# Eight experts in 144 equal weight units instead of 160, with longer rows and an unrolled loop

## The chip, the cores and the metric

One Trainium2 chip, of which one NeuronCore runs the whole kernel. The metric is the device time of one execution in microseconds (us). The kernel before ran three times: 1297.24, 1297.76 and 1300.47 us, median 1297.76 us.

## The reference

A decoder trunk of two layers makes one step for 256 prompt tokens and 8 sample tokens, 264 in all, with D = 1024. Each layer has a mixer (one wide projection, a gated linear recurrence, a short convolution, an output projection), a feed-forward part and a gated per-layer embedding. The feed-forward part of layer 0 is a dense SwiGLU; that of layer 1 sends each token to 2 of 8 experts:

```
logits = n2 @ router                      # 264 x 8, float32
top_v, top_i = top_k(logits, 2);  top_w = softmax(top_v)
for e in range(8):                        # w_gu[e]: 1024 x 3072, w_dn[e]: 1536 x 1024, float32
    g, u = split(n2 @ w_gu[e], 2)
    out += comb[:, e:e+1] * ((silu(g) * u) @ w_dn[e])
```

All weights are float32 in HBM. One expert has 18 MB of them (12 MB gate and up, 6 MB down).

## The kernel before

Each weight matrix comes through SBUF in units of at most 1 MB. A unit has four steps, each in order on one engine. SyncE (SP) issues its DMA into a raw slot (`load`, L282 to L292) as soon as that slot's last unit has been converted. ScalarE makes its float16 upper half (`hi`, L827, `wh <- raw`). VectorE makes its float16 remainder (`lo`, L1129, `wl <- raw, wh`). TensorE multiplies three times for each pair of tiles: upper by upper, upper by lower half of the activations, remainder by upper. `wh` and `wl` have four slots, so that a unit is converted at most three units ahead of TensorE (`LEAD`): `hi` of unit n + 3 waits until TensorE is done with unit n - 1.

The expert part runs from about 745 us of the profile to 1240. Before it a routing chain ranks the logits. Each expert then has a table of up to 96 tokens (`CAP`): a one-hot matrix `sel` (VectorE, L1565) gathers their activations by matmul from `nt`, where the 264 tokens lie on partitions in tiles of 128, 128 and 8 (L720, 48 matmuls). A loop (`Fori`) over the experts, one body on each engine, holds per expert:

- 12 gate and up units of 1 MB, 256 columns of all 1024 rows, so 1 KB runs in HBM. Each is 48 matmuls with 96 moving columns (L753 to L755), read out by ScalarE (L1078, L1079, L1082) and multiplied by VectorE in four operations for every two units (L1469 to L1475).
- then the gather for the next expert (L720), which TensorE runs ahead of
- 8 down units of 768 KB, 512 columns of 384 rows, 2 KB runs, 9 matmuls of 512 columns each (L782 to L784). The first four make the left half of the output, the last four the right.
- the output rows, scaled by the routing weight (`ye`: L1098 on ScalarE, L1641 on VectorE), which TensorE scatters back to the 264 tokens (L733, L735) while the next expert's gate and up units run; VectorE adds them to the residual (L1614, eight adds).

The first turn scatters zeros, and the last gathers once more for nobody: nine gathers, eight of use. Five raw slots hold the units (four of `raw`, and `xb`). The four loads of the PLE matrix that follows the experts wait for the four units before each. A pass for tables that overflow is branched over.

Of the kernel before, what the change touches and what calls it, by code (L numbers as in the profile page):

```python
# [12 lines left out]
P = 128  # L13
# [13 lines left out]
MOE_SLOTS = SLOTS + 1  # L27
# [21 lines left out]
MOE_EVAC = MOE_GU + 2  # L49
UNCOUNTED = NE * (MOE_U - MOE_EVAC)  # L50
# [35 lines left out]
def moe_unit_size(u):  # L86
    return UNIT if u % MOE_U < MOE_GU else DN_K * 512


def program(nc, a, o):  # L90

    ctx = ExitStack()
    with ctx:
# [52 lines left out]
        spare = sb("spare", [1, 5])  # L146
        csr = sb("csr", [P, 2])
        csl = sb("csl", [P, 1])
# [8 lines left out]
        raw_slot = [raw[:, i] for i in range(SLOTS)] + [xb[:].rearrange("p c t -> p (c t)")[:, 0:UNIT]]  # L157
# [13 lines left out]
        hid_e = w1_half[:, 0:2 * EC * CAP].rearrange("p (s c t) -> p s c t", s=2, c=EC)  # L171
        at = 2 * EC * CAP
# [3 lines left out]
        xg = ga[:].rearrange("p a c t -> p (a c t)")[:, 0:2 * C * CAP].rearrange("p (s c t) -> p s c t", s=2, c=C)  # L176
        sel = ga[:].rearrange("p a c t -> p (a c t)")[:, 2 * C * CAP:2 * C * CAP + 3 * CAP].rearrange("p (t n) -> p t n", t=3)
        ye = gb[:].rearrange("p a c t -> p (a c t)")[:, 0:2 * D].rearrange("p (s n) -> p s n", s=2)
        sel_t = gb[:].rearrange("p a c t -> p (a c t)")[:, 2 * D:2 * D + T]
# [11 lines left out]
        pair_u, pair_w = pair2[:, 0], pair2[:, 1]  # L191
        plew = side[:].rearrange("p a c n -> p (a c n)").rearrange("p (k n) -> p k n", k=PC)
# [28 lines left out]
        selt_full = sem("selt_full")  # L221
        sp_sel, sp_gat, sp_x, sp_csl = sem("sp_sel"), sem("sp_gat"), sem("sp_x"), sem("sp_csl")
# [40 lines left out]
        def _(sp):  # L263
# [66 lines left out]
            n0 = N_MOE  # L330
            gu = a["moe_w_gu"][0].rearrange("e (c p) m -> p e c m", p=P)
            dn = a["moe_w_dn"][0].rearrange("e (c p) m -> p e c m", p=P)
            sp.wait_ge(hi_done, N_MOE)
            sp.wait_ge(lo_done, N_MOE)
            with sp.Fori(0, NE) as e:
                for u in range(MOE_GU):
                    if u == SLOTS:
                        sp.wait_ge(aux_full, AX_LGT)
                        sp.wait_ge(xn_ready, 4 * 5)
                    col = (u % 2) * FE + (u // 2) * 256  # L340
                    load(n0 + u, gu[:, bass.ds(e, 1), :, col:col + 256].rearrange("p e c m -> p (e c) m"),
                         u % MOE_SLOTS, C, e, MOE_U, MOE_SLOTS)
                for u in range(MOE_DN):
                    half, k = u // 4, u % 4 * DN_K
                    src = dn[:, bass.ds(e, 1), k:k + DN_K, half * 512:(half + 1) * 512]
                    load(n0 + MOE_GU + u, src.rearrange("p e c m -> p (e c) m"), (MOE_GU + u) % MOE_SLOTS, DN_K, e,
                         MOE_U, MOE_SLOTS)
# [97 lines left out]
        def _(pe):  # L445
# [153 lines left out]
            def ple(l, n):  # L599
                norm_stats()  # L600
                pe.wait_ge(side_loaded, 16 * 5 * (l + 1))
                if l:
                    pe.wait_ge(sc_done, 8 * NE + 16)
# [29 lines left out]
            for t, (lo, n) in enumerate(TOK):  # L633
                last = nc.tensor.transpose(bank[0:n, t * NE:(t + 1) * NE], lgt[:, lo:lo + n], ident[0:NE, 0:NE])
            last.then_inc(aux_full, 1)

            def rows_of_tokens(s):

                for t, (lo, n) in enumerate(TOK):
# [10 lines left out]
            for t, (lo, n) in enumerate(TOK):  # L650
                last = nc.tensor.transpose(bank[0:NE, lo:lo + n], rank[0:n, t, :], ident[0:n, 0:n])
# [4 lines left out]
            for t, (lo, n) in enumerate(TOK):  # L656
                nc.tensor.transpose(bank[0:n, t * NE:(t + 1) * NE], cum[:, lo:lo + n], ident[0:NE, 0:NE])
# [5 lines left out]
            def slots_by_token(bank):  # L663

                for t, (lo, n) in enumerate(TOK):
# [4 lines left out]
            with pe.If(spilled > 0):  # L670

                with pe.Fori(0, SPILLS) as p:
                    with pe.Fori(0, NE) as e:
# [3 lines left out]
                        for c in range(C):  # L677
                            bank = aux[:, c // 4, (c % 4) * CAP:(c % 4 + 1) * CAP]
                            for i in range(6):
                                t, n = i // 2, TOK[i // 2][1]  # L680
# [31 lines left out]
            def gather(adds):  # L712

                for g in range(4):
                    pe.wait_ge(sc_done, adds(g + 5))
                    for c in (2 * g, 2 * g + 1):
                        for s in range(2):
                            at = (c % 2 * 2 + s) * CAP
                            for t, (_, n) in enumerate(TOK):
                                last = nc.tensor.matmul(aux[:, g, at:at + CAP], nt[0:n, s, t, c * P:(c + 1) * P],  # L720
                                                        sel[0:n, t, :], start=(t == 0), stop=(t == 2))
                    if g == 3:
                        for t, (_, n) in enumerate(TOK):
# [4 lines left out]
            def scatter(chunks, free):  # L728

                for c in chunks:  # L730
                    if free:
                        free(c)
                    nc.tensor.matmul(aux[:, c % 4, 0:T], ye[0:CAP, 0, c * P:(c + 1) * P], sel_t[0:CAP, :],  # L733
                                     start=True, stop=False)
                    nc.tensor.matmul(aux[:, c % 4, 0:T], ye[0:CAP, 1, c * P:(c + 1) * P], sel_t[0:CAP, :],  # L735
                                     start=False, stop=True).then_inc(sc_full, 1)

            pe.wait_ge(sel_ready, 1)
            gather(lambda i: i)
            with pe.Fori(0, NE) as e:  # L740
                pe.wait_ge(gat_done, e * 4 + 4)
                for u in range(MOE_GU):
                    n = N_MOE + u
                    pe.wait_ge(evac_done, e * MOE_EVAC + (n - 1))
                    pe.wait_ge(hi_done, e * MOE_U + (n + 1))
                    pe.wait_ge(lo_done, e * MOE_U + (n + 1))
                    th = wh[:, u % SLOTS, :].rearrange("p (c m) -> p c m", c=C)
                    tl = wl[:, u % SLOTS, :].rearrange("p (c m) -> p c m", c=C)
                    for m in range(2):
                        bank = acc[:, u % 2, m * CAP:(m + 1) * CAP]  # L750
                        for k in range(C):
                            hi, lo = th[:, k, m * P:(m + 1) * P], tl[:, k, m * P:(m + 1) * P]
                            nc.tensor.matmul(bank, hi, xg[:, 0, k, :], start=(k == 0), stop=False)  # L753
                            nc.tensor.matmul(bank, hi, xg[:, 1, k, :], start=False, stop=False)  # L754
                            last = nc.tensor.matmul(bank, lo, xg[:, 0, k, :], start=False, stop=(k == C - 1))  # L755
                    last.then_inc(unit_mm, 1)
                    if u == 1:
                        pe.wait_ge(ys_ready, e * 2 + 2)
                        pe.wait_ge(selt_ready, e + 1)
                        scatter(range(4), None)  # L760
                    if u in (4, 6):
                        scatter(range(u, u + 2), lambda i: pe.wait_ge(sc_done, e * 8 + (8 + i - 3)))
                    if u == 7:
                        pe.wait_ge(sc_done, e * 8 + (8 + 5))
                        slots_by_token(aux[:, 0, :]).then_inc(selt_full, 1)
                pe.wait_ge(sel_ready, e + 2)
                gather(lambda i: e * 8 + (i + 8))
                for u in range(MOE_DN):
                    n = N_MOE + MOE_GU + u
                    half, k0 = u // 4, u % 4 * DN_K  # L770
                    pe.wait_ge(hi_done, e * MOE_U + (n + 1))
                    pe.wait_ge(lo_done, e * MOE_U + (n + 1))
                    if k0 == 0:
                        pe.wait_ge(ys_ready, e * 2 + (half + 1))
                    th = wh[:, u % SLOTS, 0:DN_K * 512].rearrange("p (c m) -> p c m", c=DN_K)
                    tl = wl[:, u % SLOTS, 0:DN_K * 512].rearrange("p (c m) -> p c m", c=DN_K)
                    for k in range(DN_K):
                        if half == 0 and (k0 + k) % 2 == 0:
                            pe.wait_ge(hid_ready, e * 6 + (FFN_IT * 2 + (k0 + k) // 2 + 1))
                        bank = acc[0:CAP, 2 + half, :]  # L780
                        first, end = k0 + k == 0, k0 + k == EC - 1
                        nc.tensor.matmul(bank, hid_e[:, 0, k0 + k, :], th[:, k, :], start=first, stop=False)  # L782
                        nc.tensor.matmul(bank, hid_e[:, 0, k0 + k, :], tl[:, k, :], start=False, stop=False)  # L783
                        last = nc.tensor.matmul(bank, hid_e[:, 1, k0 + k, :], th[:, k, :], start=False, stop=end)  # L784
                    last.then_inc(unit_mm, 1)

            pe.wait_ge(selt_ready, NE + 1)
# [897 lines left out]
```

## Time and profile before

| | us |
|---|---|
| median of the three runs | 1297.76 |
| the profiled execution, span | 1300.5 |
| first gather of the expert part starts | 745.26 |
| last down matmul starts | 1239.63 |
| ScalarE reads the next norm's sum | 1257.05 |
| busy TensorE / VectorE / ScalarE | 1219.6 / 1021.0 / 746.0 |

The span is that of the profiled execution, within 0.03 us of the slowest of the three runs. A busy TensorE includes matmuls that overlap; the distance between starts tells its pace. In the page's 40 slices each slice is 32.5 us, so slices 24 to 38 are the expert part.

### The profile page before, as it was taken

To read this page: it belongs to the slowest core of one execution; us is meant where nothing else is said; L and a number is where in the kernel's file an instruction comes from. 1 tells how busy PE (TensorE), PEld (TensorE's weight loads), DVE (VectorE), ACT (ScalarE), POOL (GpSimd) and SP (SyncE) were. 2 spreads that over 40 slices of the span, in tenths; PEclk is the share of its full clock that TensorE was granted. 3 is DMA by queue.
4 is the path that set the end of the run, shared out by engine and by line. 5 is a ranking of instruction groups with operands and counts; after the bars stand their busy time and mean duration, and the time that the engine had idled before them with its cause. 6 is when DMAs were issued, how large, how long until landed. Compare 5 with 4: busy or idle time off the path is not lost.

```text
span 1300.5 us, 30219 instructions
## 1 busy us (share of the span) xinstructions
PE 1219.6 (94%) x12256; PEld 981.2 (75%) x12256; DVE 1021.0 (79%) x1203; ACT 746.0 (57%) x802; POOL 24.9 (2%) x59
## 2 busy tenths in 40 slices
PE   8999999999999998999999789897979798989888
PEld 4888888788888887888888476767666666767656
DVE  5977877876666689868867768979797978889875
ACT  5556644465554464466443575767676675858543
POOL 3000000000000010000000000000000000000000
PEclk9999999999999999999999988989898898989889
DMA  9675655646566543655654558989899999989720
GB/s 251 195 245 176 204 190 192 195 149 200 190 201 198 194 146 131 209 180 181 208 198 129 163 180 273 355 274 331 286 322 294 316 301 322 295 294 337 259 83 34
DMA packets 257298, 288.66 MB, mean 222 GB/s; under 512 B 5451, under 2 KB 230747, under 8 KB 257226
## 3 DMA queue, kind: packets, MB, share of 16 engines
q1 hardware_dynamic: 255514, 283.71, 67.4%
q0 software_dynamic: 1728, 4.16, 1.2%
q8 instruction: 40, 0.66, 0.2%
q14 instruction: 16, 0.13, 0.0%
HBM read 286.53 MB, written 1.52 MB: 221 GB/s over the span
## 4 chain that ended last, share of the span: by engine, by line
PE 67%; DVE 19%; issue 8%; ACT 4%; DMA 2%; DVEq 1%; ACTq 0%; SPq 0%
PE acc L496 14%; PE acc L498 14%; PE acc L497 14%; DVE wl L1129 9%; PE aux L720 5%; ACT wh L827 2%; PE acc L782 2%; PE acc L783 2%; PE acc L784 2%; PE acc L481 2%; PE acc L482 2%; PE acc L488 2%; DVE h L1614 1%; PE acc L753 1%; PE acc L755 1%
## 5 line engine op out<-in xcount | busy, mean ns | idle before, releaser
L1129 DVE SCALAR_TENSOR_TENSOR wl<-raw,wh 128x2048 f16<-128x2048 f32 (+1 forms) x252 | 548.8, 2186 | 165.9 <-ACT wh L827 163.0
L827 ACT ACTIVATE wh<-raw 128x2048 f16<-128x2048 f32 (+1 forms) x252 | 459.7, 1825 | 101.8 <-PE acc L784 61.8
L496 PE MATMUL acc<-xn,wh 128*128 128x264 f16 x1424 | 393.0, 276 | 0.8 <-DVE wl L1129 0.8
L498 PE MATMUL acc<-xn,wl 128*128 128x264 f16 x1424 | 393.0, 276 | 0.0
L497 PE MATMUL acc<-xn,wh 128*128 128x264 f16 x1424 | 393.0, 276 | 0.0
L753 PE MATMUL acc<-ga,wh 128*128 128x96 f16 x1536 | 210.0, 209 | 40.2 <-DVE wl L1129 26.4
L755 PE MATMUL acc<-ga,wl 128*128 128x96 f16 x1536 | 210.4, 210 | 0.0
L754 PE MATMUL acc<-ga,wh 128*128 128x96 f16 x1536 | 210.1, 210 | 0.0
L753 PEld LDWEIGHTS acc<-ga,wh 128*128 128x128 f16 x1536 | 153.3, 100 | 48.8 <-issue 44.3
L496 PEld LDWEIGHTS acc<-xn,wh 128*128 128x128 f16 x1424 | 139.3, 98 | 21.9 <-ACT wh L827 1.0
L497 PEld LDWEIGHTS acc<-xn,wh 128*128 128x128 f16 x1424 | 139.3, 98 | 21.1
L498 PEld LDWEIGHTS acc<-xn,wl 128*128 128x128 f16 x1424 | 139.3, 98 | 20.9
L754 PEld LDWEIGHTS acc<-ga,wh 128*128 128x128 f16 x1536 | 153.5, 100 | 0.9
L755 PEld LDWEIGHTS acc<-ga,wl 128*128 128x128 f16 x1536 | 153.6, 100 | 0.0
L862 ACT ACTIVATE ot<-acc 128x528 f32<-128x528 f32 x47 | 28.6, 610 | 124.2 <-PE acc L498 97.3
L782 PE MATMUL acc<-wh,w 128*96 128x512 f16 x192 | 80.3, 418 | 0.0
L783 PE MATMUL acc<-wl,w 128*96 128x512 f16 x192 | 79.4, 414 | 0.0
L784 PE MATMUL acc<-wh,w 128*96 128x512 f16 x192 | 78.9, 411 | 0.0
L1129 DVE SCALAR_TENSOR_TENSOR wl<-xb,wh 128x2048 f16<-128x2048 f32 (+1 forms) x32 | 64.6, 2020 | 4.2 <-ACT wh L827 4.2
L720 PE MATMUL aux<-ga,w 128*128 128x96 f16 (+1 forms) x432 | 62.1, 251 | 3.4 <-issue 3.4
L827 ACT ACTIVATE wh<-xb 128x2048 f16<-128x2048 f32 (+1 forms) x32 | 54.3, 1697 | 14.8 <-DMA xb<-in_moe_w_gu 9.8
L720 PEld LDWEIGHTS aux<-ga,w 128*128 128x128 f16 (+1 forms) x432 | 32.3, 103 | 32.7 <-issue 3.5
(268 smaller groups left out, 1611.0 us busy)
## 6 DMA issues: line engine op xcount, KB each, us to landing
raw<-in_moe_w_gu SPq DMA_DIRECT2D x80, 1024.0 KB, 8.4
raw<-in_w_in SPq DMA_DIRECT2D x56, 1024.0 KB, 5.1
raw<-in_moe_w_dn SPq DMA_DIRECT2D x48, 768.0 KB, 5.9
raw<-in_ffn_w_gu SPq DMA_DIRECT2D x24, 1024.0 KB, 5.2
xb<-in_moe_w_gu SPq DMA_DIRECT2D x16, 1024.0 KB, 8.6
raw<-in_ffn_w_dn SPq DMA_DIRECT2D x12, 1024.0 KB, 5.3
xb<-in_moe_w_dn SPq DMA_DIRECT2D x16, 768.0 KB, 6.0
raw<-in_w_a_out SPq DMA_DIRECT2D x8, 1024.0 KB, 5.1
```

What stands on the lines that cost most here:

```text
L496: nc.tensor.matmul(bank, hi, x[:, 0, x0 + k, :], start=(k == 0), stop=False)
L497: nc.tensor.matmul(bank, hi, x[:, 1, x0 + k, :], start=False, stop=False)
L498: last = nc.tensor.matmul(bank, lo, x[:, 0, x0 + k, :], start=False, stop=(k == k_chunks - 1))
L720: last = nc.tensor.matmul(aux[:, g, at:at + CAP], nt[0:n, s, t, c * P:(c + 1) * P], sel[0:n, t, :], start=(t == 0), stop=(t == 2))
L753: nc.tensor.matmul(bank, hi, xg[:, 0, k, :], start=(k == 0), stop=False)
L754: nc.tensor.matmul(bank, hi, xg[:, 1, k, :], start=False, stop=False)
L755: last = nc.tensor.matmul(bank, lo, xg[:, 0, k, :], start=False, stop=(k == C - 1))
L782: nc.tensor.matmul(bank, hid_e[:, 0, k0 + k, :], th[:, k, :], start=first, stop=False)
L783: nc.tensor.matmul(bank, hid_e[:, 0, k0 + k, :], tl[:, k, :], start=False, stop=False)
L784: last = nc.tensor.matmul(bank, hid_e[:, 1, k0 + k, :], th[:, k, :], start=False, stop=end)
L827: nc.scalar.activation(wh[:, s, 0:size], raw_slot[from_slot][:, 0:size], ACT.Copy, scale=WS).then_inc(hi_done, 1)
L1129: op(V.scalar_tensor_tensor(out=wl[:, s, 0:size], in0=raw_slot[raw_turn(n)[0]][:, 0:size], scalar=WS, in1=wh[:, s, 0:size], op0=ALU.mult, ...
```

## The change

An expert becomes 18 units of 1 MB. A gate or up unit is now 512 columns of 512 rows (2 KB runs), and two such units fill one PSUM bank with four blocks of 96 columns; a down unit is all 1024 columns of 256 rows (4 KB runs), 12 matmuls, both halves of the output together. There are six raw slots (`ya` is added). The token tiles of the expert part are 88, 88 and 88 (`MTOK`). The loop over experts is written out, with constant wait values. The gather of the next expert comes after its predecessor's second down unit, into a second copy of `xg`; the four VectorE operations for two units become two on VectorE for four units, a copy on ScalarE and a subtraction on VectorE, all 384 wide. The first turn scatters nothing and there are eight gathers. The PLE loads wait for the unit six before each. POOL's queue is not touched; on SP the wait for all earlier conversions ahead of the expert loads is gone.

```diff
-MOE_SLOTS = SLOTS + 1
+MOE_SLOTS = 6
-FFN_IT, MOE_GU, MOE_DN = FF // 512, 2 * FE // 256, 8
+FFN_IT, MOE_GU, MOE_DN = FF // 512, 12, 6
-DN_K = EC // 4
+GU_K, DN_K = C // 2, 2
+RT = T // 3
+MTOK = ((0, RT), (RT, RT), (2 * RT, RT))
-        raw_slot = [raw[:, i] for i in range(SLOTS)] + [xb[:].rearrange("p c t -> p (c t)")[:, 0:UNIT]]
+        raw_slot = [raw[:, i] for i in range(SLOTS)] + [x[:].rearrange("p c t -> p (c t)")[:, 0:UNIT] for x in (ya, xb)]
...
-            def load(n, src, slot, k, it=None, step=0, slots=SLOTS):
+            def load(n, src, slot, k, it=None, step=0):
+                slots = MOE_SLOTS if n >= N_MOE + SLOTS else SLOTS
...
-                    sp.wait_ge(hi_done, n - LEAD)
-                    sp.wait_ge(lo_done, n - LEAD)
+                    sp.wait_ge(hi_done, n + 1 - slots)
+                    sp.wait_ge(lo_done, n + 1 - slots)
...
-            sp.wait_ge(hi_done, N_MOE)
-            sp.wait_ge(lo_done, N_MOE)
-            with sp.Fori(0, NE) as e:
+            for e in range(NE):
                 for u in range(MOE_GU):
...
+                    k, col = u % 2 * GU_K, u // 2 % 2 * FE + u // 4 * 512
+                    moe_load(gu_unit(e, u), gu[:, e, k:k + GU_K, col:col + 512], GU_K)
+                for d in range(MOE_DN):
+                    moe_load(dn_unit(e, d), dn[:, e, d * DN_K:(d + 1) * DN_K, :], DN_K)
...
-                            for t, (_, n) in enumerate(TOK):
+                            for t, (_, n) in enumerate(MTOK):
                                 last = nc.tensor.matmul(aux[:, g, at:at + CAP], nt[0:n, s, t, c * P:(c + 1) * P],
                                                         sel[0:n, t, :], start=(t == 0), stop=(t == 2))
...
+            def gate_or_up(e, u):
+                n, s = gu_unit(e, u), u % 2
+                group = GROUPS * e + u // 4
+                if s == 0 and group:
+                    pe.wait_ge((gate_out, up_out)[u // 2 % 2], group)
+                if u < 2:
+                    pe.wait_ge(gat_done, 4 * e + 2 * u + 2)
+                pe.wait_ge(hi_done, n + 1)
+                pe.wait_ge(lo_done, n + 1)
...
+                for m in range(4):
+                    bank = acc[:, u // 2 % 2, m * CAP:(m + 1) * CAP]
+                    for k in range(GU_K):
...
+            for e in range(NE):
                 for u in range(MOE_GU):
+                    gate_or_up(e, u)
+                    if e and u in (2, 4):
+                        scatter(e - 1, range(2 * u - 4, 2 * u))
+                for d in range(MOE_DN):
+                    down(e, d)
+                    if e + 1 < NE and d == 1:
+                        pe.wait_ge(sel_ready, e + 2)
+                        gather(e + 1)
+                    if e + 1 < NE and d == 2:
+                        selected_slots(e + 1)
+            keep_warm(14)
+            scatter(NE - 1, range(C))
...
+            def down(e, d):                       # ScalarE
+                n = dn_unit(e, d)
+                hi(n + LEAD)
+                if d == 0:
+                    hidden_hi(GROUPS * e + GROUPS - 1)
+                if d == MOE_DN - 1:
+                    act.wait_ge(unit_mm, n + 1)
+                    act.wait_ge(csl_ready, e + 1)
...
-            op(V.memset(ye[0:CAP], 0.0), ys_ready, 2)
-            op(V.memset(sel_t[0:CAP, :], 0.0), selt_ready)
...
+            def gate_or_up(e, u):                 # VectorE
+                n, q = gu_unit(e, u), GROUPS * e + u // 4
+                lo(n + LEAD)
+                if u in (4, 8):
+                    hidden_lo(q - 1)
+                if u % 4 == 3:
...
+                    op(V.scalar_tensor_tensor(out=moe_w[:, b, :], in0=moe_t[:, b, :], scalar=1.0, in1=moe_g[:, b, :],
+                                              op0=ALU.add, op1=ALU.mult))
+                    settle()
+                    op(V.scalar_tensor_tensor(out=moe_w[:, b, :], in0=moe_w[:, b, :], scalar=0.5 * XS,
+                                              in1=moe_u[:, b, :], op0=ALU.mult, op1=ALU.mult), hid_w)
```

## Rows read from the trace of the kernel before

**Rows 1.** The page: granted clock and busy DMA share in 40 slices.

```profile
PEclk9999999999999999999999988989898898989889
DMA  9675655646566543655654558989899999989720
```

**Rows 2.** TensorE's gathers for experts 0, 1 and the last (x48), and the last down matmuls.

```profile
745.26 7.41 PE L720 MATMUL aux<-ga,w 128*128 128x96 f16 x48 [3.37 <-issue]
...
788.66 6.10 PE L720 MATMUL aux<-ga,w 128*128 128x96 f16 x48
...
1216.15 6.42 PE L720 MATMUL aux<-ga,w 128*128 128x96 f16 x48
...
1239.42 0.38 PE L783 MATMUL acc<-wl,w 128*96 128x512 f16 x1
1239.63 0.38 PE L784 MATMUL acc<-wh,w 128*96 128x512 f16 x1
```

**Rows 3.** Stretches: length, busy us by engine, granted clock, DMA share, GB/s.

```profile
870.00:896.00 26.00, 22.63 (x418) 19.72 (x415) 25.28 (x26) 20.59 (x22) 0.00 (x0) 1.00 1.10 348
897.00:901.00 4.00, 2.61 (x62) 2.49 (x60) 3.90 (x5) 3.41 (x7) 0.00 (x0) 1.00 1.07 379
862.00:864.00 2.00, 2.00 (x11) 1.11 (x10) 1.33 (x2) 1.48 (x1) 0.00 (x0) 1.00 0.00 1
908.30:921.90 13.60, 13.60 (x80) 7.44 (x78) 8.17 (x16) 3.23 (x5) 0.00 (x0) 0.50 0.90 305
```

**Rows 4.** ScalarE (start us, us, instruction): gate/up conversions, a down conversion, a gather readout.

```profile
886.53 1.91 ACT L827 ACTIVATE wh<-raw 128x2048 f16<-128x2048 f32 x1 [0.88 <-DMA raw<-in_moe_w_gu]
...
889.54 1.91 ACT L827 ACTIVATE wh<-raw 128x2048 f16<-128x2048 f32 x1 [0.67 <-DMA raw<-in_moe_w_gu]
...
859.66 1.48 ACT L827 ACTIVATE wh<-raw 128x1536 f16<-128x1536 f32 x1 [7.01 <-PE acc L784]
...
790.31 0.48 ACT L1061 ACTIVATE ga<-aux 128x384 f16<-128x384 f32 x1
```

**Rows 5.** VectorE in order of time, one of each kind.

```profile
755.49 2.29 DVE L1129 SCALAR_TENSOR_TENSOR wl<-raw,wh 128x2048 f16<-128x2048 f32 x1 [1.46 <-ACT wh L827]
760.51 2.29 DVE L1129 SCALAR_TENSOR_TENSOR wl<-xb,wh 128x2048 f16<-128x2048 f32 x1 [2.73 <-ACT wh L827]
...
847.39 0.62 DVE L1565 TENSOR_SCALAR ga<-iota,pos 128x96 f16<-128x96 f32 x3
...
872.73 4.48 DVE L1129 SCALAR_TENSOR_TENSOR wl<-raw,wh 128x2048 f16<-128x2048 f32 x2
877.13 0.74 DVE L1641 SCALAR_TENSOR_TENSOR gb<-acc,csl,gb 96x512 f16<-96x512 f32 x1
886.65 0.77 DVE L1614 SCALAR_TENSOR_TENSOR h<-aux,h 128x264 f32<-128x264 f32 x2
1271.64 0.70 DVE L1457 SCALAR_TENSOR_TENSOR ya<-ot,ya 128x528 f32<-128x528 f32 x1
```

**Rows 6.** TensorE matmul starts at full clock (784) and at half clock (909).

```profile
784.12 0.21 PE L755 MATMUL acc<-ga,wl 128*128 128x96 f16 x1
784.16 0.21 PE L753 MATMUL acc<-ga,wh 128*128 128x96 f16 x1
...
909.29 0.28 PE L754 MATMUL acc<-ga,wh 128*128 128x96 f16 x1
909.37 0.28 PE L755 MATMUL acc<-ga,wl 128*128 128x96 f16 x1
```

**Rows 7.** Instruction packets by queue (packets, MB, share of 16 engines): page, then 746:800.

```profile
q8 instruction: 40, 0.66, 0.2%
...
q8 instruction: 7, 0.11, 0.9%
```

**Rows 8.** ScalarE after the last expert.

```profile
1242.21 1.91 ACT L827 ACTIVATE wh<-raw 128x2048 f16<-128x2048 f32 x1 [1.10 <-DMA raw<-in_w_ple_gate]
1257.05 0.48 ACT L848 ACTIVATE std<-aux,eps 128x264 f32<-128x264 f32 x1 [10.84 <-PE aux L536]
```

More of the change, by code:

```diff
@@ L637, in rows_of_tokens @@
             def rows_of_tokens(s):
[L639 removed]
+                for t, (lo, n) in enumerate(MTOK):
                     bank = aux_bank().bitcast(F16)
@@ L710, in _, with gather @@
                 pe.nop()
-            def gather(adds):
+            def gather(e):
                 for g in range(4):
-                    pe.wait_ge(sc_done, adds(g + 5))
+                    if e == 1:
+                        pe.wait_ge(gat_done, g + 1)
+                    if e > 1:
+                        pe.wait_ge(sc_done, 8 * (e - 2) + 4 + g + 1)
+                    if e and g == 0:
+                        pe.wait_ge(selt_ready, e)
                     for c in (2 * g, 2 * g + 1):
@@ new lines, in down @@
+            def down(e, d):
+                n = dn_unit(e, d)
+                pe.wait_ge(hi_done, n + 1)
+                pe.wait_ge(lo_done, n + 1)
+                if d == 0 and e:
+                    pe.wait_ge(ys_ready, 2 * e)
+                if d % 2 == 0:
+                    pe.wait_ge(hid_ready, 2 * FFN_IT + GROUPS * e + d // 2 + 1)
+                th = wh[:, n % SLOTS, :].rearrange("p (c m) -> p c m", c=DN_K)
+                tl = wl[:, n % SLOTS, :].rearrange("p (c m) -> p c m", c=DN_K)
+                for k in range(DN_K):
+                    at = (d * DN_K + k) * CAP
+                    x_hi, x_lo = (hid_e[:, e % 2, i, at:at + CAP] for i in range(2))
+                    for half in range(2):
+                        cols = slice(half * 512, (half + 1) * 512)
+                        bank = acc[0:CAP, 2 + half, :]
+                        nc.tensor.matmul(bank, x_hi, th[:, k, cols], start=(d == 0 and k == 0), stop=False)
+                        nc.tensor.matmul(bank, x_hi, tl[:, k, cols], start=False, stop=False)
+                        last = nc.tensor.matmul(bank, x_lo, th[:, k, cols], start=False,
+                                                stop=(d == MOE_DN - 1 and k == DN_K - 1))
+                last.then_inc(unit_mm, 1)
@@ L738, in _ @@
+            pe.wait_ge(evac_done, N_MOE)
             pe.wait_ge(sel_ready, 1)
-            gather(lambda i: i)
-            with pe.Fori(0, NE) as e:
-                pe.wait_ge(gat_done, e * 4 + 4)
+            gather(0)
+            selected_slots(0)
+            for e in range(NE):
                 for u in range(MOE_GU):
[L743 to L785, printed above, removed]
@@ new lines, in down @@
+            def down(e, d):
+                n = dn_unit(e, d)
+                hi(n + LEAD)
+                if d == 0:
+                    hidden_hi(GROUPS * e + GROUPS - 1)
+                if d == MOE_DN - 1:
+                    act.wait_ge(unit_mm, n + 1)
+                    act.wait_ge(csl_ready, e + 1)
+                    if e:
+                        act.wait_ge(sc_full, 8 * e)
+                    for half in range(2):
+                        nc.scalar.activation(ye[0:CAP, 0, half * 512:(half + 1) * 512], acc[0:CAP, 2 + half, :],
+                                             ACT.Identity, scale=csl[0:CAP, e % 4:e % 4 + 1]).then_inc(ye_hi, 1)
@@ L1100, in _ @@
+            gathered(0)
+            selected_slots(0)
+            for e in range(NE):
+                for u in range(MOE_GU):
+                    gate_or_up(e, u)
+                for d in range(MOE_DN):
+                    down(e, d)
+                    if e + 1 < NE and d == 2:
+                        gathered(e + 1)
+                    if e + 1 < NE and d == 3:
+                        selected_slots(e + 1)
             ple(1, N_PLE[1])
@@ new lines, in down @@
+            def down(e, d):
+                n = dn_unit(e, d)
+                lo(n + LEAD)
+                if d == 0:
+                    hidden_lo(GROUPS * e + GROUPS - 1)
+                if d == MOE_DN - 1:
+                    for half in range(2):
+                        s = slice(half * 512, (half + 1) * 512)
+                        vec_e.wait_ge(ye_hi, 2 * e + half + 1)
+                        op(V.scalar_tensor_tensor(out=ye[0:CAP, 1, s], in0=acc[0:CAP, 2 + half, :],
+                                                  scalar=csl[0:CAP, e % 4:e % 4 + 1], in1=ye[0:CAP, 0, s],
+                                                  op0=ALU.mult, op1=ALU.subtract), ys_ready)
@@ L1644, in expert @@
-                settle()
-                vec_e.wait_ge(gat_done, e * 4 + 8)
-                slot_weights()
-            run_loop(NE, {lo_done: MOE_U, dv: 2 * 6 + 3 + 1, pair_free: 6, hid_ready: 6, ys_ready: 2, sc_done: 8,
-                          sel_ready: 1, csl_ready: 1}, expert)
+                for d in range(MOE_DN):
+                    down(e, d)
+                    if e + 1 < NE and d == 4:
+                        slot_weights(e + 1)
             for c in range(C):
-                add_scattered(c, lambda i: NE * 8 + i)
+                add_scattered(NE - 1, c)
```

238 lines of the change are left out of this document (122 added, 116 removed).

## The prediction

> **What bounds the kernel now.** I read the page's slices first. Through the routing TensorE runs with a granted clock near full and DMA engines about half busy; in the expert part the DMA share rises to 8 and 9 tenths, but not to a steady 9, and the clock dips once per expert [rows 1]. So something there is periodic. The gathers give the period: from 788.66 to 1216.15 are seven experts, 61.07 us each [rows 2].
>
> Next I cut one period into stretches [rows 3]. In the gate and up units DMA is saturated: share 1.10, 348 GB/s. There VectorE is busy 25.28 of 26 us, nearly full too. ScalarE says which of them ends last: it starts a unit every 3.01 us and each time waits 0.67 to 0.88 us for the DMA [rows 4]. 1.0486 MB at 348 GB/s is 3.01 us, so this part goes at the pace of 1 KB runs. In the down part ScalarE waits 7.01 us for TensorE [rows 4], no slot comes free, and DMA stands still (1 GB/s from 862 to 864 [rows 3]). TensorE there works through a gather of 6.1 to 6.4 us [rows 2] and the first down units at half clock: 908.3 to 921.9 is granted 0.50 (1.2 of 2.4 GHz) with TensorE busy 13.6 of 13.6 us [rows 3]. So an expert is a DMA-bound stage and a TensorE-bound stage one after the other, with little overlap between them. Twelve units at 3.01 are 36.1 us, eight of 0.786 MB at 379 GB/s would be 16.6, sum 52.7: some 8.4 us of the 61.07 are idle DMA.
>
> **The change part by part.**
>
> *Rows and units.* The 2 KB runs of today's down units reach 379 GB/s where the queue is full [rows 3]. The new gate and up units have such runs; down units have 4 KB runs, which no row shows alone. I price all 18 at 379: 2.77 us each, 49.8 per expert. Bounds: no gain from longer runs, 3.01 us; and for the 4 KB runs the step from 1 to 2 KB once more, 2.54 us, worth 6 x 0.23 = 1.4 per expert. I take 379, as the row of the same run length for two thirds of the bytes. The sixth slot keeps DMA at most six units ahead of VectorE.
>
> The Trainium skill, DMA: Bandwidth & Descriptors (Specifications and Bandwidth), gives about 358 GB/s as what HBM grants one core, which would speak against this gain: by it a unit takes 2.93 us, an expert 52.7, as an estimate. The trace shows 379 over 4 us, above that figure, so I keep the row.
>
> *VectorE.* Two conversions back to back take 4.48 us, the second starting 2.20 after the first (4.48 - 2.29 + overlap) [rows 5]. Per expert: 18 x 2.20 = 39.6. Hidden values: nine operations 384 wide (two multiplies and a subtraction for each of three groups); two 264-wide ones take 0.77 together and a 528-wide one 0.70, so about 0.55 each, 5.0 (bounds 9 x 0.39 = 3.5 and 9 x 0.70 = 6.3; 384 lies halfway). Four pairs of adds at 0.68 (0.77 less overlap): 2.7. Two output halves at 0.74: 1.5. The one-hot 0.62 [rows 5] and three tiny operations, together 1.2 as an estimate. Sum 50.0 us.
>
> *ScalarE.* 18 conversions at 1.91 are 34.4; nine readouts, three new copies and the gather's four, all 384 wide, at 0.48 [rows 4] add 7.7, the rest some 2: 44, below 50, so the moved copy costs nothing while VectorE or DMA is later. If it were not, it would cost 3 x 0.48.
>
> *TensorE.* The same counts, 576 gate/up and 72 down matmuls. At full clock gate/up starts are 0.04 apart [rows 6], so 23 us; down starts 0.21 apart [rows 2], 72 x 0.21 = 15.1; scatter about 2, 16 matmuls of 264 columns. The gather is 48 matmuls in 6.10 us at mostly full clock, 0.127 each, although a gate/up matmul of the same 96 columns takes 0.04. Every third one is on the 8-token tile; with three equal tiles of 88 I expect no such break and the gate/up pace: 48 x 0.04 = 1.9, between that and no gain, 6.1. Sum 42 to 46 us, below VectorE. The gather now stands after two down units; behind it on TensorE wait four down units, and ScalarE has three units converted ahead (5 to 8 us of work for TensorE), so its pause of 2 to 6 us is covered by them. If they are not there, it costs its length, as today.
>
> *New waits.* Scatter and `xg` wait for the readout of the next gather, which ended some 10 us earlier. TensorE's single-step transposes (`selected_slots`) wait one readout of 0.5 us per expert; behind it stand four down units, and I cost it at nothing for the same cover.
>
> *Unrolling.* Today's loop body is fetched once: seven 16 KB instruction packets in 746 to 800 [rows 7] and none later in the expert part. Written out, each expert fetches its own, seven times eight. Page: 40 packets are 0.2% of 16 engines' 1300.5 us, 1.04 us each. If all lie on one DMA engine, it loses 7.3 us per expert, and a unit has landed only when its slowest engine is done; if they spread, 0.45. No row names the engine. I take the middle, 3.6, since in 746 to 800 DMA waits on ScalarE were no more than half a microsecond above those of rows 4. So DMA: 49.8 + 3.6 = 53.4 per expert, 2.97 per unit.
>
> The Trainium skill, Runtime: NRT & Kernel Launch (Instruction fetch mechanics), has a taken branch break the fetch ahead and prefers unrolled code. The trace disagrees for this loop: no packet after its first turn. By the rule unrolling would gain a stall per turn; by the row it only adds packets.
>
> *The sum, on the profile's clock.* (a) First gather at 745.26, 7.41 us at half clock [rows 2]; 48 matmuls at 0.08 [rows 6] are 3.9, so all that follows it starts 3.5 earlier; VectorE's first expert conversion 755.49 [rows 5] becomes 752.0. (b) The pipeline fills: 4 us idle, as 1.46 and 2.73 before its first two conversions now [rows 5]. (c) VectorE then has 141 conversions, 310.2, and 8 x 5.0 + 7 x (2.7 + 1.5 + 1.2) = 78: its last ends at 1144, and TensorE's last unit of 2.6 at 1147. That is the floor. (d) DMA: after 18 conversions and the rest of expert 0, at 802, it can be six units ahead, at unit 26; 117 more at 2.97 end at 1149.5; conversion in two steps and the last unit, 1.9 + 2.2 + 2.6, end at 1156. So DMA is last by 9 us. (e) For half-clock stretches and the two near-equal streams meeting I add 6 us, from nothing to 8 x 6.8 = 54 (each of today's half-clock stretches of 13.6 losing half): the last down matmul ends at 1162, against 1239.9 now [rows 2]. (f) From there to the next norm's sum are 17.2 us now, with ScalarE's conversions of the PLE units waiting 1.1 us and more for loads in front of the second output half [rows 8]. These loads now start two units, some 5.5 us, sooner: I take 4, from 0 to 5.5. Sum: 78 + 4 = 82 off 1300.5: 1218.5. The median lies 2.7 below the profiled execution: 1216 us.
>
> **The rivals.**
> 1. *One engine's extra packets, or runs that gain nothing.* For it: a landing needs all 16 parts. Full 7.3 per expert: 3.17 per unit, 802 + 371 + 6.7 = 1180, with no allowance (e), since a DMA that is last by so much covers it: 18 later than 1162, so 1234. With 3.01 for every run and half the packets: 3.21, 1185, so 1239. Against: the 379 row. 1228 to 1245. By the figure of the Trainium skill (DMA: Bandwidth & Descriptors, Specifications) a unit would take 2.93 + 0.2, the stage end at 1175 and the run take 1229, the near end of this case.
> 2. *The half clock stays where it is.* For it: a gate/up unit holds TensorE 2.0 of some 2.9 us, as loose as now, and in the period of rows 3 the clock fell at the end of that stage (908.3, gather at 909); then down units take 5.1 us instead of 2.6. Per expert 13.6 us at half clock lose 6.8, and if nothing covers it period 58 to 60: 1162 + 8 x 6 = 1210, so 1264. Against: three units of cover, and the thin gather gone.
> 3. *TensorE stays at half clock through the gate/up units: slower.* Place: L753's successors, 576 x 0.08 = 46 us, with down, gather and scatter at full clock 66 per expert, above 61.07: 8 x 4.9 = 39 more in the stage, 7.5 back at its ends, 1329. It decides from 60% of the period at half clock (43 us of work plus half of 36); in rows 3 it is 13.6 of 61.07. Against: at half clock those units would leave no idle time, and after a busy stretch (908.3 to 921.9) the clock came back.
> 4. *It doesn't do what it says:* the sixth slot and longer runs wait behind TensorE's order as today: 1290 to 1300. Against: the idle DMA follows from gather and half clock, which change.
>
> **How the numbers follow.** Forecast 1200 to 1228: 0.58. Rival 1, 1228 to 1245: 0.20. Rival 2, 1245 to 1290: 0.13. Rival 4, 0.04, half of it within 0.3%. Rival 3, 0.05. Range 1198 to 1246, which leaves out rivals 2 to 4 and a part below the floor. Under 0.3%, 4 us, nothing could be told from no change. Faster 0.93, same 0.02, slower 0.05.
>
> **What would show it.** The gather's 48 matmuls in 2 to 4 us (from 6); the rate in gate/up stretches near 379 from 348; about 56 more instruction packets; gathers 52 to 55 us apart; no DMA standstill in the down units; VectorE busy over 90% of an expert. It would be wrong if ScalarE still waited several microseconds for TensorE in each expert, if waits for DMA grew past 0.9 us, or if half clock held through the gate/up units.

## The result, and the profile after

The changed kernel takes 1238.05 us (median of four runs, 1235.05 to 1239.42) against 1299.08 of the kernel before: ratio 0.9522, 95% interval 0.9500 to 0.9544. That is faster, inside the forecast range, and 22 us above the predicted 1216. It lies in the time band of rival 1, which blamed DMA; the profile shows that DMA was not the cause. The profiled execution took 1235.05 us, its span is 1233.4.

The page of the changed kernel, granted clock and DMA share in 40 slices of 30.8 us, and the instruction queues (packets, MB, share of 16 engines), against [rows 1, 7]:

```profile
PEclk8999999999999999999999998999989898989989
DMA  9675665646556654465565626999899998989900
...
q8 instruction: 79, 1.29, 0.4%
q14 instruction: 23, 0.18, 0.0%
```

The DMA share is steadier than in [rows 1], but the clock still dips in the expert part. TensorE's first gather of the expert part and a later one, the last down matmul, and then ScalarE's read of the next norm's sum, against [rows 2, 8]:

```profile
744.16 4.00 PE L739 MATMUL aux<-ga,w 88*128 88x96 f16 x48 [3.40 <-issue]
...
1054.66 2.21 PE L739 MATMUL aux<-ga,w 88*128 88x96 f16 x48
...
1173.98 0.38 PE L811 MATMUL acc<-wh,w 128*96 128x512 f16 x1
```

```profile
1188.85 0.48 ACT L887 ACTIVATE std<-aux,eps 128x264 f32<-128x264 f32 x1 [11.68 <-PE aux L550]
```

Behind the first, a gather takes 2.2 us where it took 6.1 to 7.45. Gathers 2 to 8 start at 782.8 to 1109.3, 54.4 us apart on average (before: 61.07).

One period of the changed kernel, cut into stretches as in [rows 3] (length, then busy us and count for PE, PEld, DVE, ACT and POOL, granted clock, DMA share, GB/s):

```profile
1012.00:1026.90 14.90, 12.41 (x255) 11.58 (x252) 14.83 (x13) 12.58 (x13) 0.00 (x0) 1.00 1.04 371
1026.90:1033.70 6.80, 4.24 (x40) 3.58 (x41) 5.72 (x7) 1.84 (x2) 0.00 (x0) 0.50 1.03 401
1033.70:1050.00 16.30, 14.24 (x312) 13.60 (x310) 12.63 (x16) 12.37 (x12) 0.00 (x0) 1.00 0.76 272
1050.00:1066.60 16.60, 16.34 (x119) 9.87 (x117) 16.09 (x10) 13.91 (x15) 0.00 (x0) 1.00 1.03 377
```

The gate/up units run at 371 GB/s (348 before), and the stretch with the gather and the down units, the last, is at full clock. The fault has moved to the middle of the gate/up units: 6.8 us at half clock, and behind them a stretch in which VectorE is busy 12.63 of 16.3 us and the DMA share falls to 0.76. The waits of the same period (engine, line, what for: us in total, times, longest) say who waits:

```profile
ACT w L1114 <- DVE sg L1695: 6.8, 3, 3.0
ACT sa L1126 <- PE acc L789: 5.9, 1, 5.9
PEld aux L763 <- DVE h L1673: 5.4, 2, 5.2
DVE wl L1188 <- ACT wh L866: 5.2, 2, 4.7
PE aux L763 <- DVE h L1673: 5.1, 1, 5.1
```

No row of that answer is a wait for a DMA. The first row is ScalarE waiting for VectorE, the slower of the two. The chain of waits puts the other four in order (start us, us, what):

```profile
1026.39 2.20 DVE wl L1188
1028.59 0.47 DVE w L1680
1029.06 0.35 DVE h L1673
1029.46 0.40 PE aux L763
...
1033.72 0.08 PE acc L789
1034.65 0.36 issue
1035.02 0.49 ACT sa L1127
1035.50 1.81 ACT wh L866
1037.33 2.21 DVE wl L1188
```

Read it from the top. TensorE finishes gate/up unit 4 (counted from 0) at 1024.4 and has the second half of the scatter (L763) next. That half writes the four `aux` banks of the first half, so it waits until VectorE has added the first half to `h` (L1673). VectorE comes to the adds only at 1029, after the conversions for units that lie up to three ahead. TensorE stands 5.1 us, its clock falls to half, and the unit behind the scatter takes 3.4 us (1031.2 to 1034.6) where the two units before it took 2.1 each. Meanwhile ScalarE and VectorE have used up their lead of three units, and VectorE then stands 4.7 us, its one long gap in the period: the 49.3 us that it is busy in the four stretches and its 5.2 us of waits make 54.5 of the 54.6 us of this period.

The kernel before had this wait too, but short: its adds stand in pairs after gate/up units 2, 3, 5 and 7, and its scatter in three pieces. TensorE's waits for the adds from 800 to 1150, in the kernel before:

```profile
PE aux L733 <- DVE h L1614: 8.4, 6, 1.6
```

and in the changed kernel:

```profile
PE aux L763 <- DVE h L1673: 34.5, 7, 5.1
```

### The profile page after: what moved, and what is told of

It is laid out like the page before. It is cut to its first block, busy times and chain, and to the rows that moved or that the text cites. A ratio compares the mean times of both kernels' runs of the same rounds, so it can differ in the third digit from the quotient of the medians.

```text
span 1233.4 us, 28154 instructions
## 1 busy us (share of the span) xinstructions
PE 1150.7 (93%) x12177; PEld 955.8 (77%) x12177; DVE 988.4 (80%) x1050; ACT 735.8 (60%) x730; POOL 24.9 (2%) x59
## 4 chain that ended last, share of the span: by engine, by line
PE 58%; DVE 32%; ACT 8%; issue 2%; DMA 0%; ACTq 0%; SPq 0%; DVEq 0%
DVE wl L1188 21%; PE acc L510 15%; PE acc L512 15%; PE acc L511 15%; ACT wh L866 5%; PE acc L495 2%; PE acc L502 2%; PE acc L496 2%; DVE h L1673 1%; DVE xb L1262 1%; PE aux L599 1%; DVE sg L1695 1%; DVE sg L1692 1%; PE aux L550 1%; DVE gb L1707 1%
## 5 line engine op out<-in xcount | busy, mean ns | idle before, releaser
L1188 DVE SCALAR_TENSOR_TENSOR wl<-raw,wh 128x2048 f16<-128x2048 f32 x220 | 501.7, 2288 | 141.2 <-ACT wh L866 140.3
L866 ACT ACTIVATE wh<-raw 128x2048 f16<-128x2048 f32 x220 | 418.1, 1906 | 4.5 <-PE acc L811 4.4
L786 PE MATMUL acc<-ga,wh 128*128 128x96 f16 x1536 | 207.6, 210 | 13.6 <-ACT wh L866 9.4
L788 PE MATMUL acc<-ga,wh 128*128 128x96 f16 x1536 | 207.2, 210 | 0.2 <-issue 0.2
L789 PE MATMUL acc<-ga,wl 128*128 128x96 f16 x1536 | 207.0, 209 | 0.4 <-issue 0.4
L809 PE MATMUL acc<-wh,w 128*96 128x512 f16 x192 | 73.2, 381 | 4.1 <-ACT wh L866 3.4
L810 PE MATMUL acc<-wl,w 128*96 128x512 f16 x192 | 72.8, 379 | 0.0
L811 PE MATMUL acc<-wh,w 128*96 128x512 f16 x192 | 72.8, 379 | 0.0
L1188 DVE SCALAR_TENSOR_TENSOR wl<-xb,wh 128x2048 f16<-128x2048 f32 x24 | 54.8, 2285 | 0.4 <-ACT wh L866 0.4
L1188 DVE SCALAR_TENSOR_TENSOR wl<-ya,wh 128x2048 f16<-128x2048 f32 x24 | 54.8, 2284 | 0.3 <-ACT wh L866 0.3
L763 PE MATMUL aux<-gb 96*128 96x264 f16 x64 | 20.6, 342 | 36.3 <-DVE h L1673 35.2
L866 ACT ACTIVATE wh<-ya 128x2048 f16<-128x2048 f32 x24 | 45.7, 1903 | 0.7 <-PE acc L789 0.7
```

The lines of the kernel that those rows point to most:

```text
L786: nc.tensor.matmul(bank, hi, x_hi, start=(s == 0 and m == 0 and k == 0), stop=False, skip_group_check=True)
L788: nc.tensor.matmul(bank, hi, x_lo, start=False, stop=False, skip_group_check=True)
L789: last = nc.tensor.matmul(bank, lo, x_hi, start=False, stop=end, skip_group_check=True)
L809: nc.tensor.matmul(bank, x_hi, th[:, k, cols], start=(d == 0 and k == 0), stop=False)
L810: nc.tensor.matmul(bank, x_hi, tl[:, k, cols], start=False, stop=False)
L811: last = nc.tensor.matmul(bank, x_lo, th[:, k, cols], start=False, stop=(d == MOE_DN - 1 and k == DN_K - 1))
```

## Experiments

Two theories stood against each other. Theory W (the wait of the scatter's second half): the place of the adds sets the period, through the scatter's wait, TensorE's stop and its clock. The rival: DMA, by fetch packets or run length, sets it, as rival 1 of the prediction has it. A third question was which part of the change made it faster at all.

**e1: the adds two units earlier.**

```diff
-                    if e and u in (4, 6):
-                        for c in range(2 * u - 8, 2 * u - 4):
+                    if e and u in (2, 5):
+                        for c in range(0, 4) if u == 2 else range(4, 8):
```

> VectorE's eight adds of the last expert come after gate/up units 2 and 5 instead of 4 and 6; nothing else changes. Theory W (the wait of the second scatter half for the first adds, 5.1 us in the trace of after, makes the one VectorE gap of 4.7 us per expert): the gap goes, 7 x 4.7 = 33 us, so 1203 to 1210 us, gathers 50 us apart, and no half clock after the scatter. Theory F (DMA with the packets of the unrolled code sets the pace near 53.4 per expert): ScalarE starts to wait for DMA and the time stays at 1228 or above. Theory C (the clock halves in any case because gate/up units are loose): half-clock stretches stay, 1220 to 1230.

Measured 1203.16 us (1202.11 to 1203.46), ratio 0.9256 (0.9240 to 0.9271): 34.9 below the changed kernel, from moving eight small instructions. The period is 49.77 us in every expert. The same stretch of time in the changed kernel:

```profile
800.00:1150.00 350.00, 301.00 (x4670) 248.41 (x4668) 314.26 (x276) 260.01 (x243) 0.00 (x0) 0.94 0.95 350
```

and in e1:

```profile
800.00:1150.00 350.00, 318.51 (x4941) 258.30 (x4938) 346.02 (x301) 282.37 (x262) 0.00 (x0) 1.00 1.01 372
```

VectorE goes from 314.26 to 346.02 busy of 350, the clock from 0.94 to 1.00. The scatter no longer stops TensorE; the first matmul of its second half follows the unit before it at once:

```profile
957.69 0.21 PE L789 MATMUL acc<-ga,wl 128*128 128x96 f16 x1
957.73 0.28 PE L763 MATMUL aux<-gb 96*128 96x264 f16 x1
```

Theory W holds. The run also bears out a term of the prediction: the period is VectorE's sum. DMA is busy all the time here too (share 1.01), but no row of the run's waits is for a DMA, so VectorE is the later of the two.

**e2: the stop stays, the clock does not fall.** Filler matmuls fill TensorE's wait.

```diff
+                    if e and u == 4:
+                        pe.wait_ge(ys_ready, 2 * e)
+                        for _ in range(24):
+                            nc.tensor.matmul(acc[:, 2, :], identh[:], identh[:, 0:1].to_broadcast([P, 512]),
+                                             start=True, stop=True)
```

> As after, but TensorE runs 24 filler matmuls of 512 columns (5.1 us at full clock) into a free bank just ahead of the second scatter half, in the time it waits anyway. Theory W says that the stop itself and the half clock that follows share the 4.7 us: at full clock the next gate is done some 1.5 to 2.5 us sooner, so 7 x 2 = 14 less, 1222 to 1230. If the half clock is the whole cause: 1203 to 1212. If it costs nothing: 1238.

Measured 1224.15 us (1223.19 to 1225.15), ratio 0.9422 (0.9407 to 0.9438). Waits from 800 to 1150:

```profile
ACT sa L1131 <- PE acc L789: 29.5, 7, 4.2
DVE wl L1193 <- ACT wh L871: 24.1, 13, 3.0
```

The period is 52.90, with full clock in all of it. Of the 4.64 us that the changed kernel loses per expert (54.41 less 49.77), 1.5 are the half clock and 3.1 the stop itself. Work that is useless but keeps TensorE busy paid here, though not as well as removing the stop.

**e3: the loop of the kernel before written out, nothing else.**

```diff
-            with pe.Fori(0, NE) as e:
+            for e in range(NE):
```

(likewise on SyncE, ScalarE and VectorE)

> The kernel before with nothing but its loop over the experts written out on all four engines. Theory F (all extra instruction packets on one DMA engine, about 1 us each): its DMA-bound gate/up units go from 3.01 to about 3.2 us, ScalarE's waits for DMA grow by 0.2 to 0.4 us each, 8 x 2.4 to 4.9 us, so 1318 to 1338. If packets spread or are absorbed: 1299 within 4. If loop turns cost something (register waits): up to 8 less, 1291.

Measured 1294.46 us (1292.00 to 1300.88, ten runs) against 1300.21, ratio 0.9959 (0.9944 to 0.9975): slightly faster. Instruction queue from 800 to 1140 in this kernel, where the kernel before has no packet:

```profile
q8 instruction: 32, 0.52, 0.7%
```

So the packets come, some six per expert, and cost nothing that can be measured; the fetch theory falls. The Trainium skill, Runtime: NRT & Kernel Launch (Instruction fetch mechanics), has a taken branch break the fetch ahead where its target is not in the two pages held; the kernel before fetches nothing from 800 to 1140, so no run here shows that stall. The 5.75 us gained, some 0.7 per turn, stay without a cause: the mean granted clock from 800 to 1150 is higher as well, 0.93 against 0.91.

**e4 and e5: four raw slots instead of six,** on the changed kernel and on e1.

```diff
-MOE_SLOTS = 6
+MOE_SLOTS = 4
...
```

> As after with four raw slots instead of six (the expert units use the same slots as the other matrices). Theory W: VectorE and the scatter wait set the pace, and three loads in flight of 2.7 us each still run ahead of a unit every 3.0 us: 1236 to 1246. Theory F (DMA is near the bound): DMA falls idle when a slot is late and cannot catch up, 1255 to 1290.

> The adds early (as e1) and four raw slots (as e4). If four slots cost e4's 18.8 us only by making the scatter wait longer (7.2 us there, from 5.2): with that wait gone nothing is left, 1203 to 1207 us. If they cost by idle DMA engines (ScalarE's waits for DMA of 0.6 to 1.7 us in e4): some 1.5 to 3 us per expert stay, 1214 to 1227.

e4 took 1256.86 us (1256.07 to 1260.05), ratio 0.9680 (0.9659 to 0.9700); e5 took 1224.04 (1221.11 to 1229.72), ratio 0.9422 (0.9385 to 0.9459). e4 is above the 1236 to 1246 that theory W had for it and inside the 1255 to 1290 of theory F, by which DMA falls idle when a slot is late and cannot catch up: a miss, as I had not counted that with four slots DMA becomes late too. e5 lies in the 1214 to 1227 of the reading by which idle DMA is what fewer slots cost. Waits of e4 from 800 to 1150:

```profile
PE aux L763 <- DVE h L1673: 40.9, 6, 7.1
...
ACT wh L866 <- DMA raw<-in_moe_w_gu: 22.9, 35, 1.4
```

and of e5:

```profile
ACT wh L866 <- DMA raw<-in_moe_w_gu: 36.5, 45, 3.1
```

The last two of the six slots are worth 19 us in the changed kernel and 21 in e1: with four, ScalarE waits for loads, with six no row of either run's waits is for a load. The kernel before had five slots, and no run prices the one that the change added.

**e6: one of the hidden operations from VectorE to GpSimd,** on e1.

```diff
+            for q in range(GROUPS * NE):
...
+                pool.wait_ge(hid_hi, q + 1)
+                nc.gpsimd.tensor_tensor(hid_e[:, r, 1, at:at + 4 * CAP], moe_w[:, q % 2, :],
+                                        hid_e[:, r, 0, at:at + 4 * CAP], ALU.subtract).then_inc(hid_ready, 1)
...
-                vec_e.wait_ge(hid_hi, q + 1)
-                op(V.tensor_tensor(hid_e[:, r, 1, at:at + 4 * CAP], moe_w[:, q % 2, :], hid_e[:, r, 0, at:at + 4 * CAP],
-                                   ALU.subtract), hid_ready)
...
```

> As e1, but the three hidden_lo subtractions of an expert (0.55 us each on VectorE) run on GpSimd. If VectorE's own work is now the bound (period 49.77, its sum was 50.0): it falls by 1.65, and DMA is next at some 48.4 (12 x 2.74 + 6 x 2.58): 8 x 1.4 = 11 less, 1190 to 1195. If DMA or ScalarE's waits for VectorE (L1114, 2.5 us each) already end last: 1201 to 1204. If GpSimd slows VectorE or its results come late: above 1204.

Measured 1206.62 us (1205.87 to 1207.04), ratio 0.9274 (0.9247 to 0.9301): 3.5 above e1, although VectorE has 3 x 0.55 us less to do per expert. GpSimd's operation, ScalarE's conversion behind the copy, and VectorE's two conversions beside them:

```profile
913.16 2.35 POOL L457 TENSOR_TENSOR w<-sg,w 128x384 f16<-128x384 f32 x1 [24.79 <-ACT w L1119]
```

```profile
912.99 1.90 ACT L871 ACTIVATE wh<-raw 128x2048 f16<-128x2048 f32 x1
```

```profile
912.45 2.28 DVE L1193 SCALAR_TENSOR_TENSOR wl<-raw,wh 128x2048 f16<-128x2048 f32 x1
914.92 2.73 DVE L1193 SCALAR_TENSOR_TENSOR wl<-raw,wh 128x2048 f16<-128x2048 f32 x1 [0.19 <-ACT wh L871]
```

The subtraction left VectorE's queue, but two things eat more than it took. VectorE now comes to its next conversion before ScalarE has converted that unit (until 914.89), and starts it 2.47 us behind the last one instead of 2.20. And it takes 2.73 us instead of 2.28, with GpSimd still running for its first 0.6 us. Together that is 0.7 us for a saving of 0.55, in two of an expert's three groups; the period is 50.27 (e1: 49.77). The conversion already running when GpSimd starts takes its usual 2.28 us, and GpSimd ends 0.8 us after it. The Trainium skill, SBUF — State Buffer (SBUF: two separate sides), calls the port pair that VectorE and GpSimd share an exclusive lock, held for a whole instruction by whoever starts first, where VectorE's operation has two inputs in SBUF as this conversion has; the 0.45 us and GpSimd's late end fit it, the wait for ScalarE is another thing. No run has GpSimd's operation alone.

**e7: only the token tiles of 88, on the kernel before.**

```diff
+RT = T // 3
+MTOK = ((0, RT), (RT, RT), (2 * RT, RT))
...
-                            for t, (_, n) in enumerate(TOK):
+                            for t, (_, n) in enumerate(MTOK):
...
```

> The kernel before with nothing but token tiles of 88, 88, 88 in the expert part. The gather (6.1 us) takes 2.0 to 2.1 as in after, in the stage in which TensorE ends last: 8 x 4 = 32 less, and a little more if half clock shrinks with it: 1258 to 1272. If the gather was covered: 1295 to 1301. In between if DMA then idles less but the half clock stays: 1275 to 1290.

Measured 1267.23 us (1266.21 to 1270.42), ratio 0.9748 (0.9717 to 0.9779): 33.6 us from one tile size. What ends last there changes too; waits of e7 from 800 to 1150:

```profile
ACT wh L829 <- DMA raw<-in_moe_w_gu: 54.5, 64, 2.0
...
ACT wh L829 <- PE acc L786: 14.3, 14, 2.6
```

and of the kernel before:

```profile
ACT wh L827 <- PE acc L784: 49.7, 18, 7.6
...
ACT wh L827 <- DMA raw<-in_moe_w_gu: 29.3, 42, 0.9
```

ScalarE's wait for TensorE in the down units shrinks from 49.7 to 14.3 us, and its largest is now the one for the loads with 1 KB rows, 54.5 us where it was 29.3.

**e8: e1 with gate/up loads in 1 KB runs.** It loads other weights of the same size into the same places.

```diff
-                    k, col = u % 2 * GU_K, u // 2 % 2 * FE + u // 4 * 512
-                    moe_load(gu_unit(e, u), gu[:, e, k:k + GU_K, col:col + 512], GU_K)
+                    moe_load(gu_unit(e, u), gu[:, e, :, u * 256:(u + 1) * 256], C)
```

> As e1, but each gate/up unit reads 256 columns of all 1024 rows (1 KB runs, as before) into the same slot: the same bytes, other weights in the places of the computation. If run length sets DMA's rate: 12 x 3.01 + 6 x 2.58 = 51.6 per expert, 1.8 above the period of 49.77, so 1214 to 1220 and waits of ScalarE for DMA in gate/up units. If run length is worth nothing: 1201 to 1205.

Measured 1219.42 us (1218.23 to 1220.15), ratio 0.9371 (0.9343 to 0.9399). One period of e1 and the same 49.8 us of e8:

```profile
933.60:983.40 49.80, 45.51 (x720) 37.30 (x719) 49.18 (x44) 40.56 (x38) 0.00 (x0) 1.00 1.03 382
```

```profile
933.60:983.40 49.80, 43.56 (x676) 34.91 (x675) 46.76 (x39) 39.64 (x37) 0.00 (x0) 1.00 1.06 362
```

DMA moves 362 GB/s in e8 at a share of 1.06, and ScalarE waits for it again, from 800 to 1150:

```profile
ACT wh L865 <- DMA raw<-in_moe_w_gu: 19.9, 25, 1.1
```

With these rows 18.87 MB per expert take 52 us, above VectorE's 50.0, and e8's gathers 2 to 8 are 51.8 us apart; with 2 and 4 KB rows the loads fit under VectorE. So in e1 the row length is worth 16 us. In the changed kernel, where a period is 54.4, no run tests it.

**e9 and e10: the old token tiles back,** in the changed kernel and in e1.

```diff
-MTOK = ((0, RT), (RT, RT), (2 * RT, RT))
+MTOK = TOK
...
```

> The changed kernel with the token tiles 128, 128 and 8 back, so a gather of some 6 us in place of 2.0; order, units, slots and the written-out loop stay. Covered theory (the down units' lead hides the gather, as the prediction's TensorE step says): the period stays near 54.4 and only the first gather, which nothing hides, is 2 to 3.5 us longer: 1239 to 1244. Uncovered theory (the shorter gather was needed in the new place too): 4.1 us longer per expert, 7 times, with or without more half clock: 1267 to 1292. In the changed kernel the worst stop is the scatter's, some 20 us later; if the gather's stop is only partly hidden, 1245 to 1265.

> The same tiles of 128, 128 and 8 with the adds after gate/up units 2 and 5, where VectorE is busy without a gap at a period of 49.8 us. TensorE has 42 to 46 us of work per expert there, so 4.1 more make it 46 to 50, up to VectorE's own 50.0. Covered theory: 1203 plus 2 to 3.5 for the first gather, 1204 to 1208. Uncovered: a VectorE gap of 1 to 4 us per expert, 1210 to 1236, and half clock back around the gather.

e9 took 1287.69 us (1286.80 to 1289.20), ratio 0.9914 (0.9897 to 0.9931); e10 took 1243.98 (1242.85 to 1244.84), ratio 0.9571 (0.9555 to 0.9587). e9 lies in the uncovered theory's 1267 to 1292. e10 lies above that theory's 1236: VectorE stands 4.5 and 0.7 us per expert (period 54.8, 5.0 above e1) where I had at most 4. The covered theory is out in both. A gather of e10, all engines in order of time:

```profile
955.37 5.42 PE L739 MATMUL aux<-ga,w 128*128 128x96 f16 x48
...
960.68 2.28 DVE L1189 SCALAR_TENSOR_TENSOR wl<-xb,wh 128x2048 f16<-128x2048 f32 x1
...
961.04 0.66 PE L809 MATMUL acc<-wh,w 128*96 128x512 f16 x1
...
965.55 1.91 ACT L866 ACTIVATE wh<-raw 128x2048 f16<-128x2048 f32 x1 [3.86 <-PE acc L811]
...
967.50 2.29 DVE L1189 SCALAR_TENSOR_TENSOR wl<-raw,wh 128x2048 f16<-128x2048 f32 x1 [4.53 <-ACT wh L866]
```

When the gather starts at 955.4, VectorE has work until 963.0: 7.6 us of cover. What must pass before it gets more is the gather with the small matmuls behind it (5.7), the next down unit (4.4, from 961.0 to 965.5, most of it at half clock) and ScalarE's conversion (2.0): 12.1, so 4.5 are missing. In e1 the gather and the unit behind it take 4.9 us (933.6 to 938.5) and with the conversion 6.9, under 7.6: there TensorE is in time, and the 0.47 us for which VectorE stands come from ScalarE's own queue, which converts only at 939.7, behind the readout of the gather. The clock in e10, before and behind the end of the gather:

```profile
955.00:961.00 6.00, 6.00 (x54) 3.68 (x52) 5.96 (x6) 5.08 (x6) 0.00 (x0) 1.00 1.04 375
961.00:964.40 3.40, 3.40 (x9) 1.68 (x10) 1.97 (x1) 0.70 (x3) 0.00 (x0) 0.51 1.05 395
```

The profile records TensorE busy for all of the 6 us before its clock fell. But the ends of matmuls are modelled, and the starts of the gather's 48 lie 0.11 us apart, where they lie 0.04 apart in e1. The two edits together (medians, us; the kernel before had 1299.1 to 1300.9 in these runs):

| | adds after units 4 and 6 | adds after units 2 and 5 |
|---|---|---|
| tiles 128, 128, 8 | 1287.69 | 1243.98 |
| tiles 88, 88, 88 | 1238.05 | 1203.16 |

Tiles are worth 49.6 or 40.8, the place of the adds 43.7 or 34.9. All the rest of the change (units, rows, slots, order, unrolling) is worth 11.6 without the tiles, and none of that is won in the period: the gathers 2 to 8 of e9 are 61.3 us apart, those of the kernel before 61.2. In e9 VectorE has both stops in each expert, 5.4 us behind the scatter's wait and 5.7 behind the gather, and each has a half-clock stretch of its own.

## Why the prediction was right or wrong, point by point

- **What bounds the kernel before: right.** The TensorE-bound gather and the DMA-bound gate/up units were the two stages, as e7 shows: the shorter gather alone takes most of the first away and leaves the second.
- **Rows and units: right in size.** 379 GB/s was the price; e1 holds 382 over a whole period, and the changed kernel has 401 in a stretch where down units are loaded. The Trainium skill's 358 GB/s for one core (DMA: Bandwidth & Descriptors, Specifications) is exceeded over e1's whole period.
- **VectorE: right.** 50.0 us were worked out; e1's period is 49.77, with VectorE busy for 49.2 of it, and its last down matmul starts at 1142.7 where step (c) put the floor at 1147.
- **Gather, TensorE: right in size, wrong in value.** 48 matmuls at the gate/up pace, 1.9 us (3.9 the first), became 2.2 and 4.0. But I took a gather of up to 6 us to be covered by three converted units, and so credited its shortening with 3.5 us at the start alone. e9 and e10 put 40.8 to 49.6 us on it. The cover is 7.6 us in e10, and the gather, the unit behind it and a conversion must pass in it, at whatever clock the gather leaves.
- **New waits: the step that failed.** I wrote that the scatter waits for the readout of the gather and costed that at nothing; the scatter's wait for the adds, 1.4 us on average in the kernel before, I did not count at all. The scatter's second half waits for VectorE's first adds, which the change put after unit 4 and the scatter's second half too; the wait is 5.1 us, makes VectorE stand 4.7, and costs 4.64 per expert against e1; for the seven experts that scatter beside gate/up units that is 32.5.
- **Unrolling and step (d): wrong.** 3.6 us per expert for fetch packets made DMA the last in the forecast. e3 finds no cost, and in the changed kernel no period waits for DMA.
- **Step (e): right in kind, not in size.** I allowed 6 us for half clock and the meeting of two streams. One half-clock stretch per expert remained, and e2 prices it at 1.5 us, 10.6 in all, part of the 32.5. That the allowance is of this size is luck: the stretch follows the scatter's stop, which the sum did not have.
- **Step (f): half right.** From the last down matmul's end to the next norm's sum: 17.2 before, 13.2 forecast, 14.5 measured.

The errors partly cancelled, and it is luck that the time still lies in the range: the step that failed costs 32.5 us, more than the 30 from the forecast to the range's end. On the profile's clock: the floor was 4 us too high, and the 9 us of DMA and the 6 of (e) stand where the 32.5 belong, so the last down matmul ended at 1174.4 instead of 1162. That is 12.4 of the 14.9 us by which the span exceeds 1218.5; the tail is 1.3 more and the rest of the kernel 1.1. The other 7 of the 22 lie between span and median: this kernel's median is 4.7 above its span (the profiled execution took 1.65 us more than its span and was the fastest of the four), where I took 2.7 off.

**The rivals.** Rival 1 named the time (1228 to 1245) and a cause that e3 and the waits exclude. Rival 2, half clock staying, is the nearest in mechanism, but at a new place and with half of the stretch. Rivals 3 and 4 did not come. Of the announced signs those of the gather, the rate, the period of 52 to 55 us, the down units without a DMA standstill (1.03) and VectorE's 90%, if barely (49.3 of the 54.6 us of a period), came; of fetch packets there are 39 more on that queue, not 56. The first sign that was to show the forecast wrong came as well: ScalarE waits 5.9 us for TensorE in each expert.

## What to carry to other kernels

When an in-order engine gets a wait on a buffer that another engine must free, find that engine's instruction in its own queue and count what stands ahead of it; being "ten microseconds earlier" for one operand says nothing of the others. A lead of n units covers a stop only if the stop, the unit behind it at the clock that the stop leaves, and the first step of the refill together are shorter than the slowest engine's n units. The worths of two repairs need not add up: here each was worth 9 us less beside the other than alone, so try a part of a change both without and with the rest.

## What the runs showed of the hardware that was not expected

- TensorE's granted clock can fall to half behind a stretch for which the profile records it busy without a gap: in e10 behind 48 matmuls of a gather in 5.4 us, not behind the same 48 in 2.2 us (e1). The two differ in their token tiles, every third with 8 rows between two of 128, or all with 88.
- VectorE's conversion beside a GpSimd operation of 384 columns takes 2.73 us instead of 2.28 (e6).
- Over a period with 2 and 4 KB rows this core's DMA moved 382 GB/s, with 1 KB rows for two thirds of the bytes 362.
